# Projection pieces moved from behind the scores to the end of an attention step

## The chip, the cores and the metric

One core of a Trainium2 chip runs the kernel, in float32. The metric is device time in microseconds (us). TensorE multiplies (its weight loads run beside it), VectorE (DVE) and ScalarE (ACT) work on vectors, SyncE's queue (SP) starts the loads of the large weights, and GpSimd's queue (POOL) those of some small parameters. Each engine works through its own instructions in order and waits on semaphores for the others.

## What is computed

Two transformer layers run over 256 latent tokens and 256 context tokens of width 1024. The part that matters here is the token mixer of a layer:

```python
p = h @ w_in[l]                       # 2560 columns: q, k, v, u, g
s = einsum('bqhmd,bkhmd->bhmqk', q, k) * scale
pr = softmax(s)                       # two maps per head
w = pr[:, :, 0] - lam * pr[:, :, 1]
a = einsum('bhqk,bkhe->bqhe', w, v)   # then RMS norm per head
mixed = einsum('gpq,bcqge->bcpge', w_s, layernorm(g)) + b_s
o = concat([a, u * mixed]) @ w_out[l]
```

Beside it, modulation vectors `silu(c) @ ada_w[l]` are needed, then a dense SwiGLU (layer 0) or a mixture of 8 experts (layer 1).

## The kernel before

**Stages.** The work goes layer by layer: norm, projection of q, k and v, attention, output projection, feed-forward part or experts. Weights come as units of 512 KB through a ring of 8 buffers (`raw`). ScalarE rounds a unit to `w_hi` (L897), VectorE makes the rest `w_lo` (L1196), and each product is made of three matmuls (L493 to L495, helper `mm3`).

**Attention steps.** `attend(l)` exists once for each engine, as a software pipeline over steps t. An item is a pair of a block of 128 queries and a head: 16 items in layer 0 and 8 in layer 1. In layer 0 the first 8 items are of context queries with 256 keys ("short" here), all others have 512 keys ("long"). The loop has two steps more than items. In step t TensorE does, in this order:

1. the scores of item t (L641), which wait for both exponentials of item t-1, since there is one pair of banks for scores
2. `project_ug(l, t)`: half of the projection of one block of u or g, 12 matmuls (L493 to L495)
3. the turn of the modulation chunk of step t-1 (L530 for gates, L534 for others), which waits for the copy `arow`
4. the transposes of the weights of item t-1 (L659), which wait for VectorE's `weights`
5. the product of item t-2 with v (L669)
6. the rows of the modulation chunk of step t (`ada_rows`, L519); if the chunk before was a gate chunk of layer 0, they wait until it is finished on VectorE (L1242, L1243)
7. in some steps a mix of the spatial gating (L624)

Modulation chunks stand in 14 of the 16 steps of layer 0 (not in 7 and 15) and in 6 of the 8 of layer 1 (not in 3 and 7).

VectorE does in step t: the softmax weights of item t-1 (L1380 to L1383), the row maximum of item t (L1389, L1390), the finish of the chunk of step t-1, the copy of the product of item t-2 (L1397), in two steps of each layer the `w_lo` of two units, the copy `arow` of the chunk of step t (L1232), which waits for its rows, and then in some steps a gate (L1366), layer norm statistics (L1330, L1331), a spatial norm (L1338 to L1341) or a head norm with a root on ScalarE (L1438 to L1448). ScalarE copies a finished block of u or g (L1015) at the start of every other step, then does the exponentials of item t (L1022), in two steps the `w_hi` of two units, the copy of the transposed weights (L1033) and a square (L1040).

GpSimd's queue loads the bias and gain of the next gate chunk (`ab_bc`, `pg_bc`) once the gate chunk before is finished. SyncE's queue gives the next 512 KB unit to a ring buffer once its old unit was used. The loads of the experts' weights start when layer 1's attention is normed (semaphore `cat1`).

Of the kernel before, what the change touches and what calls it, by code (L numbers as in the profile page):

```python
# [95 lines left out]
def spread(t, c0, c1, steps):  # L96

    c = c0 + -(-t * (c1 - c0) // steps)
    return c if 0 <= t < steps and -(-(t + 1) * (c1 - c0) // steps) > c - c0 else None


def ada_slot(l, t):

    if l == 0:
        return spread(t, 4, ADA_L1, NB * HEADS)
    return spread(t, ADA_L1, 24, NLAT * HEADS)
# [60 lines left out]
def program(nc, x, c, ctx, c_ctx, ada_w, ada_b, pre_mix_g, post_mix_g, pre_ffn_g, post_ffn_g, w_in, w_out,  # L167
# [6 lines left out]
    with ExitStack() as stack:  # L174
        def sem(name):
            return stack.enter_context(nc.semaphore(name))
# [102 lines left out]
        def sg(name):  # L279

            if name not in S:
                S[name] = sem(name.replace(" ", "_"))
            return S[name]

        def view(ring, u):
            return ring.rearrange("p (k n) -> p k n", k=u.shape[0])
# [26 lines left out]
        def out_blocks(l):  # L313
            return range(NB) if l == 0 else range(NLAT)
# [176 lines left out]
        def _(pe):  # L491
            def mm3(o, lh, ll, rh, rl, start, stop):
                pe.matmul(o, lh, rh, start=start, stop=False)  # L493
                pe.matmul(o, lh, rl, start=False, stop=False)  # L494
                return pe.matmul(o, ll, rh, start=False, stop=stop)  # L495

            def split_at(s):
                return w_hi[:, s % SPL, :], w_lo[:, s % SPL, :]
# [7 lines left out]
            def ada_rows(c, bank, which=range(4)):  # L506

                if c and which[0] == 0:
                    if two_gates(c - 1):
                        pe.wait_ge(sg("ada fin"), c)  # L510
                    else:
                        pe.wait_ge(sg("arow"), c)
                for u in [at["ada", c][i] for i in which]:
                    pe.wait_ge(raw_in[u.k % RAW], raw_count(u.k))
                    w = view(raw_at(u.k), u)
                    for kk in range(2):
                        k = 2 * (u.a % 4) + kk
                        q = k % 4
                        m = pe.matmul(ps[32 * q:32 * q + 32, bank, :], cstat[:, k, :], w[:, kk, :],  # L519
                                      start=(k < 4), stop=(k >= 4), tile_position=(0, 32 * q))  # L520
                    m.then_inc(ada_used, 1)

            def ada_turn(c, bank):

                pe.wait_ge(sg("arow"), c + 1)
                if c:
                    pe.wait_ge(sg("ada fin"), c)
                if ADA_SEQ[c][1] in (2, 5):
                    for r in streams(ADA_SEQ[c][0]):
                        m = pe.matmul(ps[:, bank + 1 - r, :], cst[:, C_SELB + P * r:C_SELB + P * r + P], arow[:, :],  # L530
                                      start=True, stop=True)
                else:
                    for j in range(4):
                        m = pe.matmul(ps[:, bank + 1, 2 * j:2 * j + 2], arow[:, P * j:P * j + P], cst[:, C_SELC:C_SELC + 2],  # L534
                                      start=True, stop=True)
                m.then_inc(sg("ada post"), 1)
# [48 lines left out]
            def spatial_weights(l):  # L585

                pe.wait_ge(sg("ws in"), 16 * (l + 1))
                for g in range(4):
                    m = pe.transpose(ps[:, BANK_MIX, P * g:P * g + P], ws_raw[:, P * g:P * g + P], ident)
                m.then_inc(sg("wsT ps"), 1)  # L590

            def project_ug(l, f):

                c = f // 2
                nb = len(out_blocks(l))
                j, b = ug[l][c]
                bank = BANK_UG + c % 2 if c < nb else BANK_UG
                if f == 0:
                    pe.wait_ge(sg("qkT%d" % l), len(qk[l]))
                elif f == 2:  # L600
                    pe.wait_ge(sg("wsT"), l + 1)
                elif f % 2 == 0:
                    pe.wait_ge(sg("proj%d" % l), proj_n[l][2] + (c if c > nb else c - 1))
                for u in at["in", l, j][2 * (f % 2):2 * (f % 2) + 2]:
                    pe.wait_ge(lo_done, u.s + 1)
                    h, lo = (view(t, u) for t in split_at(u.s))
                    for kk in range(2):
                        k = 2 * at["in", l, j].index(u) + kk
                        m = mm3(ps[:, bank, :], hT_hi[:, k, P * b:P * b + P], hT_lo[:, k, P * b:P * b + P],
                                h[:, kk, :], lo[:, kk, :], k == 0, k == KD - 1)  # L610
                    if b == out_blocks(l)[-1]:
                        m.then_inc(unit_used, 1)
                if b < out_blocks(l)[-1]:
                    if f % 2:
                        m.then_inc(sg("ug part"), 1)

            def mix(l, i):

                b = out_blocks(l)[i]
                pe.wait_ge(sg("vn%d" % l), i + 1)  # L620
                if i:
                    pe.wait_ge(sg("gated"), NB * l + i)
                for g in range(4):
                    m = pe.matmul(ps[:, BANK_MIX, P * g:P * g + P], wsT[:, P * g:P * g + P],  # L624
                                  proj[:, b, 4 * DA + P * g:4 * DA + P * g + P], start=True, stop=True)
                m.then_inc(sg("mixed"), 1)

            def attend(l):
                its = items[l]
                n = len(its)  # L630
                for t in range(n + 2):
                    if t < n:
                        b, h = its[t]
                        k0 = 0 if b < NLAT else 256
                        if t == 0:
                            pe.wait_ge(sg("proj%d" % l), proj_n[l][1] + 2)
                            pe.wait_ge(sg("qkT%d" % l), len(qk[l]) if l else len(qk[l]) - 2 * NLAT)
                        else:
                            pe.wait_ge(sg("exp%d" % l), 2 * t)
                        for m_ in range(2):  # L640
                            m = pe.matmul(ps[:, m_, 0:512 - k0], qT[l][HD * m_:HD * m_ + HD, h, P * b:P * b + P],  # L641
                                          kT[HD * m_:HD * m_ + HD, h, k0:512], start=True, stop=True)
                        m.then_inc(sg("scores%d" % l), 1)
                        project_ug(l, t)
                    if t == 0:
                        spatial_weights(l)
                    if ada_slot(l, t - 1):
                        ada_turn(ada_slot(l, t - 1), ADA)
                    if 1 <= t <= n:
                        i = t - 1  # L650
                        b, h = its[i]
                        nk = 4 if b < NLAT else 2
                        pe.wait_ge(sg("weights%d" % l), i + 1)
                        if i:
                            pe.wait_ge(sg("wT%d" % l), i)
                        else:
                            pe.wait_ge(sg("proj%d" % l), proj_n[l][2])
                        for kb in range(nk):
                            m = pe.transpose(ps[:, BANK_W, P * kb:P * kb + P], pr[:, i % 2, 0, P * kb:P * kb + P], ident)  # L659
                        m.then_inc(sg("wT ps%d" % l), 1)  # L660
                    if t >= 2:
                        i = t - 2
                        b, h = its[i]
                        kb0, nk = (0, 4) if b < NLAT else (2, 2)
                        pe.wait_ge(sg("wT%d" % l), i + 1)
                        if i:
                            pe.wait_ge(sg("o%d" % l), i)
                        for kb in range(nk):
                            m = pe.matmul(ps[:, BANK_O, 0:P], wT[:, i % 2, P * kb:P * kb + P],  # L669
                                          proj[:, kb0 + kb, 2 * DA + P * h:2 * DA + P * h + P], start=(kb == 0), stop=(kb == nk - 1))  # L670
                        m.then_inc(sg("pv%d" % l), 1)
                    if ada_slot(l, t):
                        ada_rows(ada_slot(l, t), ADA)
                    if t in MIX_AT[l]:
                        mix(l, MIX_AT[l].index(t))
# [982 lines left out]
```

## Time and profile before

| what | value |
|---|---|
| median of 3 runs | 1927.09 us (1927.06 to 1927.76) |
| profiled execution, its time and its span | 1922.89 us, 1921.0 us |
| mean granted TensorE clock | 0.962 |
| TensorE busy | 1768.6 us (92%) |
| VectorE busy | 1331.0 us (69%) |
| ScalarE busy | 1099.1 us (57%) |

The span runs from the first to the last instruction. A share of busy time is a mean over all stages. Attention of layer 0 runs from 130 to 275 us, that of layer 1 from 786 to 863 us.

### The profile page before, as it was taken

How to read it: one execution, taken by the hardware profiler on the slowest of the kernel's cores; microseconds unless marked ns; L12 is line 12 of the kernel's file. 1: busy time of each engine (PE TensorE's matmuls, PEld its weight loads, DVE VectorE, ACT ScalarE, POOL GpSimd, SP SyncE). 2: the span in 40 equal slices, each digit the busy share in tenths (PEclk: the TensorE clock that was granted, in tenths of full speed). 3: DMA queues.
4: the chain of work that ended last, by engine and by line, in shares of the span. 5: the costliest groups of instructions: out<-in, count | busy, mean ns of one | idle time of the engine just before them, and what ended most of it. 6: DMA issues, size and time to landing. Idle time of an engine off the chain costs nothing.

```text
span 1921.0 us, 24495 instructions
## 1 busy us (share of the span) xinstructions
PE 1768.6 (92%) x8208; PEld 1412.8 (74%) x8208; DVE 1331.0 (69%) x1595; ACT 1099.1 (57%) x1408; POOL 26.6 (1%) x45
## 2 busy tenths in 40 slices
PE   5899988999999979978599999999999999999993
PEld 1775567788888857646488888888888888888883
DVE  1445765443333455474599999999999999999994
ACT  2333434322222244344487888878888888888883
POOL 2000000000000000000000000000000000000000
PEclk7899999999999989997799999999999999999997
DMA  9438762534443323564599999999999999999992
GB/s 310 154 121 278 254 208 88 182 125 162 134 132 99 95 59 99 175 208 154 196 394 371 376 388 359 395 368 381 383 362 394 366 381 389 360 394 363 382 384 91
DMA packets 232655, 504.91 MB, mean 263 GB/s; under 512 B 15672, under 2 KB 38352, under 8 KB 232320
## 3 DMA queue, kind: packets, MB, share of 16 engines
q1 hardware_dynamic: 229312, 493.49, 71.3%
q0 software_dynamic: 3264, 10.39, 1.9%
q8 instruction: 46, 0.75, 0.2%
q14 instruction: 33, 0.27, 0.0%
HBM read 496.48 MB, written 19.92 MB: 269 GB/s over the span
## 4 chain that ended last, share of the span: by engine, by line
issue 52%; PE 37%; DVE 6%; DMA 2%; ACT 2%; POOL 0%; SPq 0%; POOLq 0%; ACTq 0%; DVEq 0%
PE ps L493 11%; PE ps L495 10%; PE ps L494 10%; PE ps L519 2%; DMA raw<-in_ada_w 1%; DVE w_lo L1196 1%; DMA pg_bc<-in_post_ffn_g 1%; PE ps L641 1%; PE ps L669 1%; PE ps L534 1%; PE ps L543 1%; DVE xs L1309 1%; DVE hT_lo L1283 0%; DVE gg L1243 0%; DVE gg L1242 0%
## 5 line engine op out<-in xcount | busy, mean ns | idle before, releaser
L1196 DVE TENSOR_TENSOR w_lo<-raw,w_hi 128x1024 fp32r<-128x1024 f32 x570 | 685.2, 1223 | 298.6 <-ACT w_hi L897 264.2
L1109 ACT ACTIVATE w_hi<-raw 128x1024 fp32r<-128x1024 f32 x448 | 473.8, 1061 | 106.7 <-PE ps L495 106.7
L493 PE MATMUL ps<-w_hi,he_hi 128*128 128x512 f32 x896 | 354.6, 396 | 0.7 <-DVE he_lo L1528 0.7
L495 PE MATMUL ps<-w_hi,he_lo 128*128 128x512 f32 x896 | 350.4, 391 | 0.0
L494 PE MATMUL ps<-w_lo,he_hi 128*128 128x512 f32 x896 | 349.8, 390 | 0.0
L1196 DVE TENSOR_TENSOR w_lo<-raw_more,w_hi 128x1024 fp32r<-128x1024 f32 x224 | 273.9, 1225 | 45.7 <-ACT w_hi L1109 26.3
L1109 ACT ACTIVATE w_hi<-raw_more 128x1024 fp32r<-128x1024 f32 x224 | 237.8, 1063 | 53.5 <-PE ps L495 53.5
L897 ACT ACTIVATE w_hi<-raw 128x1024 fp32r<-128x1024 f32 x122 | 128.7, 1063 | 214.3 <-PE ps L495 214.3
L495 PEld LDWEIGHTS ps<-w_hi,he_lo 128*128 128x128 f32 x896 | 168.8, 188 | 36.1
L493 PEld LDWEIGHTS ps<-w_hi,he_hi 128*128 128x128 f32 x896 | 169.0, 189 | 34.9 <-issue 1.0
L494 PEld LDWEIGHTS ps<-w_lo,he_hi 128*128 128x128 f32 x896 | 169.0, 189 | 33.9
L493 PE MATMUL ps<-w_hi,ae_hi 128*128 128x512 f32 x448 | 175.2, 391 | 5.6 <-DVE ae_lo L1547 5.6
L495 PE MATMUL ps<-w_hi,ae_lo 128*128 128x512 f32 x448 | 174.4, 389 | 0.0
L494 PE MATMUL ps<-w_lo,ae_hi 128*128 128x512 f32 x448 | 174.4, 389 | 0.0
L493 PE MATMUL ps<-w_hi,hT_hi 128*128 128x512 f32 x368 | 151.0, 410 | 22.2 <-DVE hT_lo L1427 6.6
L494 PE MATMUL ps<-w_lo,hT_hi 128*128 128x512 f32 x368 | 146.7, 399 | 0.0
L495 PE MATMUL ps<-w_hi,hT_lo 128*128 128x512 f32 x368 | 146.6, 398 | 0.0
L493 PE MATMUL ps<-hT_hi,w_hi 128*128 128x512 f32 x352 | 137.8, 391 | 6.0 <-DVE hT_lo L1283 6.0
L494 PE MATMUL ps<-hT_lo,w_hi 128*128 128x512 f32 x352 | 137.7, 391 | 0.0
L495 PE MATMUL ps<-hT_hi,w_lo 128*128 128x512 f32 x352 | 137.6, 391 | 0.0
L493 PEld LDWEIGHTS ps<-w_hi,hT_hi 128*128 128x128 f32 x368 | 71.5, 194 | 54.0 <-issue 24.0
L493 PEld LDWEIGHTS ps<-w_hi,ae_hi 128*128 128x128 f32 x448 | 84.1, 188 | 24.8 <-issue 3.4
(206 smaller groups left out, 1950.3 us busy)
## 6 DMA issues: line engine op xcount, KB each, us to landing
raw<-in_moe_w SPq DMA_DIRECT2D x448, 512.0 KB, 6.1
raw_more<-in_moe_w SPq DMA_DIRECT2D x224, 512.0 KB, 6.1
raw<-in_ada_w SPq DMA_DIRECT2D x96, 512.0 KB, 6.0
raw<-in_ffn_w SPq DMA_DIRECT2D x66, 512.0 KB, 3.8
raw<-in_w_in SPq DMA_DIRECT2D x40, 512.0 KB, 3.8
raw<-in_w_out SPq DMA_DIRECT2D x16, 512.0 KB, 7.7
yrows<-in_x SPq DMA_DIRECT2D x8, 512.0 KB, 6.8
xe<-xrows SPq DMA_DIRECT2D x8, 512.0 KB, 6.6
```

Source lines behind the costliest of these rows:

```text
L493: pe.matmul(o, lh, rh, start=start, stop=False)
L494: pe.matmul(o, lh, rl, start=False, stop=False)
L495: return pe.matmul(o, ll, rh, start=False, stop=stop)
L519: m = pe.matmul(ps[32 * q:32 * q + 32, bank, :], cstat[:, k, :], w[:, kk, :], start=(k < 4), stop=(k >= 4), tile_position=(0, 32 * q))
L534: m = pe.matmul(ps[:, bank + 1, 2 * j:2 * j + 2], arow[:, P * j:P * j + P], cst[:, C_SELC:C_SELC + 2], start=True, stop=True)
L543: m = pe.transpose(ps[:, k, P * b:P * b + P], xn[:, b, P * k:P * k + P], ident)
L641: m = pe.matmul(ps[:, m_, 0:512 - k0], qT[l][HD * m_:HD * m_ + HD, h, P * b:P * b + P], kT[HD * m_:HD * m_ + HD, h, k0:512], start=True, s ...
L669: m = pe.matmul(ps[:, BANK_O, 0:P], wT[:, i % 2, P * kb:P * kb + P], proj[:, kb0 + kb, 2 * DA + P * h:2 * DA + P * h + P], start=(kb == 0) ...
L897: act.activation(w_hi[:, u.s % SPL, :], raw_at(u.k), ACT.Copy).then_inc(hi_done, 1)
L1109: act.activation(w_hi[:, s % SPL, :], expert_raw(i), ACT.Copy).then_inc(hi_done, 1)
L1196: dve.tensor_tensor(w_lo[:, s_ % SPL, :], src, w_hi[:, s_ % SPL, :].bitcast(F32), ALU.subtract)\
L1309: dve.scalar_tensor_tensor(out=xs[:, b, :], in0=src[:, b, :], scalar=st[:, 28 + b:29 + b], in1=xs[:, b, :], op0=ALU.mult, op1=ALU.add).the ...
```

## The change

In every step but step 0 of a layer, TensorE's piece of the projection of u and g (12 matmuls) is issued behind the product with v instead of behind the scores. In step 0 it stays. Nothing changes on the other engines, and no instruction is added or removed.

```diff
                         m.then_inc(sg("scores%d" % l), 1)
+                    if t == 0:
                         project_ug(l, t)
-                    if t == 0:
                         spatial_weights(l)
                     if ada_slot(l, t - 1):
                         ada_turn(ada_slot(l, t - 1), ADA)
...
                         m.then_inc(sg("pv%d" % l), 1)
+                    if 1 <= t < n:
+                        project_ug(l, t)
                     if ada_slot(l, t):
                         ada_rows(ada_slot(l, t), ADA)
                     if t in MIX_AT[l]:
```

## Rows read from the trace of the kernel before

**Rows 1.** Windows: stretch, busy us of PE, PEld, DVE, ACT, POOL, then clock, DMA.

```profile
125.00:330.00 205.00, 181.52 (x1026) 126.29 (x1025) 124.37 (x288) 78.56 (x193) 5.03 (x9) 0.98 0.61 209
...
900.00:1921.00 1021.00, 966.29 (x4377) 799.89 (x4375) 895.08 (x837) 789.22 (x829) 7.75 (x8) 0.97 0.95 353
```

**Rows 2.** Timeline of TensorE, steps 4 and 7 of layer 0: start us, us, instruction.

```profile
165.76 0.70 PE L641 MATMUL ps<-kT,qT 64*128 64x256 f32 x4
166.39 0.50 PE L493 MATMUL ps<-w_hi,hT_hi 128*128 128x512 f32 x1
...
169.24 0.95 PE L534 MATMUL ps<-cst,arow 128*128 128x2 f32 x8
170.05 0.41 PE L659 MATMUL ps<-cst,pr 128*128 128x128 f32 x2
...
190.07 1.88 PE L530 MATMUL ps<-arow,cst 128*128 128x512 f32 x4
```

**Rows 3.** Timeline of VectorE in the same step 4.

```profile
165.92 0.69 DVE L1232 COPY arow<-ps 128x512 f32<-128x512 f32 x1 [1.62 <-PE ps L519]
...
167.35 0.48 DVE L1383 SCALAR_TENSOR_TENSOR pr<-pr,att 128x256 f32<-128x256 f32 x1
```

**Rows 4.** Waits of TensorE from 130 to 863 us: who for whom, us, times, longest.

```profile
PE ps L659 <- DVE pr L1383: 8.1, 4, 5.7
PE ps L519 <- DVE gg L1243: 6.8, 3, 2.6
PE ps L493 <- DVE w_lo L1196: 4.2, 3, 2.5
...
PE ps L493 <- ACT proj L1015: 2.8, 2, 1.6
```

**Rows 5.** Windows behind four waits of TensorE: the clock stands after POOL.

```profile
147.00:149.00 2.00, 2.00 (x18) 0.56 (x15) 0.12 (x1) 0.00 (x0) 1.08 (x2) 1.00 0.18 57
...
196.20:199.40 3.20, 3.19 (x8) 2.52 (x9) 3.09 (x6) 0.00 (x0) 0.65 (x1) 0.50 0.76 212
...
211.90:216.30 4.40, 4.40 (x21) 0.92 (x21) 1.66 (x7) 2.73 (x7) 1.07 (x2) 0.64 1.00 318
...
855.30:859.00 3.70, 2.82 (x12) 2.53 (x12) 0.83 (x4) 1.00 (x3) 0.00 (x0) 0.60 0.00 0
```

**Rows 6.** Timeline of TensorE, step 13 of layer 0.

```profile
240.55 1.13 PE L641 MATMUL ps<-kT,qT 64*128 64x512 f32 x4
...
246.23 0.66 PE L659 MATMUL ps<-cst,pr 128*128 128x128 f32 x4 [0.80 <-DVE pr L1383]
...
249.56 1.16 PE L624 MATMUL ps<-proj,wsT 128*128 128x128 f32 x8
```

**Rows 7.** Timeline of VectorE: statistics, head norm, then step 13 of layer 0.

```profile
173.47 0.68 DVE L1330 BATCH_NORM_STATS2 st<-proj 128x6 f32<-128x512 f32 x1
...
174.40 0.17 DVE L1380 RECIPROCAL att<-att 128x2 f32<-128x2 f32 x1
...
180.41 0.16 DVE L1438 TENSOR_SCALAR st<-st 128x4 f32<-128x4 f32 x1
...
182.32 0.16 DVE L1380 RECIPROCAL att<-att 128x2 f32<-128x2 f32 x1
...
241.32 1.12 DVE L1366 SCALAR_TENSOR_TENSOR proj<-ps,pcol,proj 128x128 f32<-128x128 f32 x4
242.36 0.15 DVE L1338 RECIPROCAL st<-st 128x1 f32<-128x1 f32 x1
...
244.46 0.16 DVE L1380 RECIPROCAL att<-att 128x2 f32<-128x2 f32 x1
...
245.43 0.75 DVE L1383 SCALAR_TENSOR_TENSOR pr<-pr,att 128x512 f32<-128x512 f32 x1
```

**Rows 8.** The page's costliest groups: busy us, mean ns of one.

```profile
L1196 DVE TENSOR_TENSOR w_lo<-raw,w_hi 128x1024 fp32r<-128x1024 f32 x570 | 685.2, 1223 | 298.6 <-ACT w_hi L897 264.2
```

**Rows 9.** DMA issues from 140 to 160 us: KB each, us from issue to landing.

```profile
pg_bc<-in_post_mix_g POOLq DMA_DIRECT2D x1, 256.0 KB, 6.3
```

## The prediction

> **What bounds the kernel now.** I read the windows by stage first. In the attention stage of layer 0 TensorE is busy for 181.5 of 205 us, VectorE for 124.4, ScalarE for 78.6 [rows 1]. So TensorE sets the pace there, and time is won or lost only where it waits. I then read its timeline step by step. A step of layer 0 is dense: scores 0.63 us to the next instruction, projection 2.85, turn 0.81 [rows 2], then transposes, product with v and rows of the chunk. What matters is where VectorE stands meanwhile. It copies `arow` 0.16 us into the step, since the chunk's rows end the step before, and its last instruction of the softmax weights ends 2.07 us into the step (167.83 less 165.76) [rows 2, 3]. The transposes need these weights. Now they come at 4.29 us, behind the projection, and find them ready. The list of TensorE's waits shows what is left: 6.8 us for a gate chunk's finish, 8.1 for weights, 4.2 for `w_lo`, 2.8 for ScalarE's copy of a block of u or g [rows 4].
>
> **What the change removes.** The same waits, part by part.
> - The gate's finish (6.8 us in steps 1, 2 and 9 of layer 0): the turn now comes ahead of the projection, so VectorE finishes the gate under 2.85 us of projection.
> - `w_lo` and the copy of u or g (4.2 + 2.8 us): the projection that needs them starts later.
> - The weights in the steps behind the last item, and the two small ones (8.1 us): the last projection now stands right ahead of these transposes. What is left of them I count as new.
> - Three of these waits dropped the granted clock: 3.2 us at 0.50, 4.4 us at 0.64, 3.7 us at 0.60 [rows 5], which cost 1.6 + 1.6 + 1.5 = 4.7 us of full speed.
>
> Sum removed: 6.8 + 8.1 + 4.2 + 2.8 + 4.7 = 26.6 us. Work of TensorE, VectorE and ScalarE is the same, instruction for instruction.
>
> **What it adds: a wait for the weights in nearly every step.** In front of the transposes now stand only scores and turn. If W is the time from the start of the step to the end of the weights, TensorE waits W less scores and turn. Scores and turn are 0.63 + 0.81 = 1.44 us in a short step and 1.13 + 0.81 = 1.94 in a long one, where the scores take 1.13 [rows 2, 6]; a gate turn of layer 0 takes 1.88 instead of 0.81 [rows 2]. VectorE can't come earlier: the weights of item t-1 are queued behind `arow`, whose rows are still the last but one thing of the step before, and behind whatever small job stands after `arow`.
>
> W is put together from VectorE's rows. Base: 2.07 us short; long 2.5 (arow 0.16 + 0.6, then 246.18 less 244.46 = 1.72) [rows 3, 7]. Jobs between `arow` and the weights: statistics 0.93, head norm 1.91, gate 1.04, spatial norm 2.10 [rows 7]. A mix at the end of the step before hides 1.16 [rows 6].
>
> Layer 0, wait of TensorE in us:
> - steps 3 and 5 (statistics): 3.0 - 1.44 = 1.6 each; step 4: 0.6; step 6 (head norm): 4.0 - 1.44 = 2.5; step 7 (statistics, gate turn): 3.0 - 0.63 - 1.88 = 0.5
> - step 2: weights ready, but the next gate's parameters aren't. They are asked for when the first gate is done, 2 us ahead of the step by then, and take 6.3 us [rows 9] and their issue; then the gate takes about 2.6 us, while the rows could start at 6.2: 1.5
> - step 8: VectorE has a gate, two `w_lo` (1.22 us each [rows 8]) and the weights ahead: W about 3.8, no turn: 2.7. Step 9 has two more `w_lo`, statistics and a gate turn: W about 4.1, less 3.0, and 0.3 for its gate: 1.4
> - step 10 (head norm): 4.4 - 1.94 = 2.5; step 11 (spatial norm): 4.6 - 1.94 = 2.7; step 12 (norm less mix): 1.5; step 13 (gate and norm): 5.6 - 1.94 = 3.7; step 14 (norm and head norm less mix): 3.4; step 15 (gate): 1.6
>
> Sum: 1.5 + 1.6 + 0.6 + 1.6 + 2.5 + 0.5 + 2.7 + 1.4 + 2.5 + 2.7 + 1.5 + 3.7 + 3.4 + 1.6 = 27.8 us. Step 13 can be checked against today's trace: the transposes wait for the weights there already, for 0.80 us behind 2.85 of projection [rows 6]; 0.80 + 2.85 = 3.65.
>
> Layer 1: steps 1 and 2: 0.6 each; 3 (statistics): 1.5; 4 (two `w_lo`, no turn): 2.7; 5: 1.6; 6 (head norm): 2.5; 7 (norm): 2.7; 8: 1.5 of today's 5.7. Sum 13.7 us. Together 41.5 us.
>
> **The clock.** Behind waits of 2.5, 2.0 and 5.7 us the clock fell; behind the longest gate wait, 2.6 us, it stayed at 1.00 [rows 5]. Nine of the new waits are 2.4 us or longer (steps 6, 8, 10, 11, 13, 14; in layer 1 steps 4, 6, 7). The rows leave open which of them cost; the bounds are none of nine (0) and all (9 x 1.6 = 14.4 us). I take half, 7.2, since of the three rows in that size (2.0, 2.5, 2.6) two fell and one did not.
>
> **Queues.** No DMA moves in its queue. Ring buffers of u and g units come free later by 2 to 4 us; their successors are output weights and chunks that are used a step or more later. GpSimd's parameter loads start earlier, with the gates. Costed at nothing; if the cover were gone, what is shown for step 2 is the size. ScalarE's copy of u or g starts later but still ahead of the exponentials, and the exponentials end about 3 us behind the weights, while TensorE has product, projection and rows, over 5 us, to do.
>
> **Sum.** 41.5 + 7.2 - 26.6 = 22.1 us slower. The profiled execution would go from 1922.9 to 1945.0 us, its span from 1921.0 to 1943.1. The median shown is 4.2 us above the profiled execution; on it the forecast is 1927.1 + 22.1 = 1949 us. The experts' stage passes the delay on whole: its loads are started by the end of layer 1's attention (`cat1`), and TensorE is busy for 966 of 1021 us [rows 1].
>
> **Rivals.**
> - *The clock falls behind every wait of 1.4 us or more.* Against it: the clock stood at 1.00 behind 2.6 us. For it: a wait in each step is a new pattern, which no row shows. Then 9 more waits count and the other half of the nine: 13.5 x 1.6 = 22 us more, 1971 us. The Trainium skill (TensorE: Matmul & The Clock Gate, "A second HAM failure mode: psum-queue depth-cycling") tells of a kernel in which frequent short pauses between groups of matmuls made the clock swing between its levels; by that rule this rival holds, and the trace of before neither shows nor excludes it. Chance 0.08.
> - *Faster: VectorE reaches the weights ahead of its side jobs.* If each new wait were only its base (0.6 us; 2.7 in the two steps with `w_lo` and no turn, 1.5 in step 2), the new waits would be about 19 us against 26.6 removed: 1919 us. It decides where the mean new wait of some 22 steps falls below 1.2 us. For it: W is read from one schedule, and gates are finished earlier in the new one. Against: each side job waits for something behind `arow` or stands behind it in program order. Chance 0.05.
> - *Hidden later.* The delay goes into slack of the experts' stage, where DMA engines are busy for 0.95 of the time [rows 1], 1927 us. Against: those loads start with the delayed signal, and their work is not shortened. Chance 0.03.
>
> **How the numbers follow.** The likeliest case has 0.84. Its ends: no clock loss and 3 us less of new waits, 1927.1 + 41.5 - 3 - 26.6 = 1939; all nine losses and 3 us more, 1927.1 + 41.5 + 3 + 14.4 - 26.6 = 1959. I put the range at 1938 to 1962, a little into the clock rival, which leaves about 0.18 outside. A measurement can tell 0.2% (3.9 us) from no change. Slower: 0.84 + 0.08 = 0.92; same 0.03; faster 0.05.
>
> **What would show it.** TensorE's waits at L659 for `pr` of L1383 rise from 8.1 to some 38 us, in about 20 places, the largest (3.7 us) in step 13 of layer 0. Those at L519 for the gate fall from 6.8 to about 2, those of L493 in the steps for `w_lo` and the copy to nothing. Step 4 of layer 0 grows from 6.9 to 7.6 us, step 1 shrinks by 2.7. The mean clock in both attention stages falls. Layer 0's attention ends some 15 us later, layer 1's adds 5 to 10, and the stages between and after keep their length. The forecast is wrong if the weights end earlier in the step than 2 us short or 2.5 long, if the clock follows another rule than half of the long waits, or if the stages behind change.

## The result, and the profile after

| | before | changed |
|---|---|---|
| median | 1927.07 us (4 runs, 1926.53 to 1927.76) | 1949.31 us (4 runs, 1948.11 to 1955.09) |
| ratio | | 1.0121, 95% interval 1.0100 to 1.0142 |
| span of the profiled execution | 1921.0 us | 1946.6 us |

The kernel became slower by 22.2 us; 22.1 was forecast. The interval of the ratio reaches from 19 to 27 us, so an agreement to 0.1 us is chance. The line numbers of the changed kernel are 2 higher from the new lines on (L1385 is L1383 of before, L1245 is L1243, L1234 is L1232).

Where the 25.6 us between the two profiled executions lie is seen in windows that end at the same instructions: the first scores of layer 0, its first output projection, the first scores of layer 1, its first output projection, the end. (The first window begins 0.4 us earlier in the changed kernel.) The changed kernel (window, length, busy us of PE, PEld, DVE, ACT, POOL, clock, DMA):

```profile
129.90:300.90 171.00, 138.04 (x773) 88.98 (x773) 94.59 (x236) 57.59 (x150) 5.01 (x9) 0.92 0.63 214
300.90:808.90 508.00, 478.48 (x2120) 395.57 (x2120) 226.03 (x303) 164.51 (x248) 0.00 (x0) 0.97 0.37 117
808.90:892.30 83.40, 65.60 (x372) 40.05 (x372) 51.82 (x112) 34.12 (x80) 3.20 (x6) 0.97 0.60 202
892.30:1946.60 1054.30, 994.69 (x4493) 822.88 (x4493) 914.30 (x874) 802.91 (x857) 8.62 (x9) 0.96 0.94 348
```

The same windows of the kernel before:

```profile
130.30:279.60 149.30, 128.67 (x773) 82.56 (x773) 95.17 (x236) 57.90 (x150) 5.03 (x9) 0.98 0.71 245
279.60:786.00 506.40, 476.83 (x2122) 394.46 (x2122) 226.12 (x303) 164.56 (x248) 0.00 (x0) 0.98 0.37 118
786.00:867.00 81.00, 66.19 (x373) 42.20 (x373) 52.35 (x112) 34.48 (x80) 3.21 (x6) 0.95 0.60 208
867.00:1921.00 1054.00, 993.87 (x4493) 822.23 (x4493) 914.37 (x874) 802.65 (x856) 8.65 (x9) 0.97 0.94 348
```

Layer 0's attention takes 21.7 us more, layer 1's 2.4, the stage between 1.6 and the experts 0.3. VectorE's and ScalarE's busy time is unchanged; TensorE's rose by 9.4 us in layer 0 at the same 773 matmuls. Most of that is the clock: 0.98 before, 0.92 now. The rest stands around the waits, where an instruction counts as busy a little longer (step 4 below).

How much of such a difference is chance can be read from the experiments, where the same code was profiled again. Layer 1's attention with unchanged code took 81.0 us in the kernel before and 83.2 in the one that is late in layer 0 only. The stage between took 506.4 us before and 511.7 in the one that is late in layer 1 only, whose code up to there is that of before. So the 2.4 and 1.6 us are within what one execution differs from another, and the 21.7 us are far beyond it (unchanged code: 149.3 and 150.0).

The list of TensorE's waits from 130 to 885 us of the changed kernel (who for whom, us, times, longest) answers to [rows 4]:

```profile
PE ps L659 <- DVE pr L1385: 34.4, 21, 3.6
...
PE ps L519 <- DVE gg L1245: 1.5, 1, 1.5
...
PE ps L534 <- DVE arow L1234: 0.8, 4, 0.2
PE ps L530 <- DVE arow L1234: 0.4, 2, 0.2
```

The waits for the weights rose from 8.1 to 34.4 us, those for a gate fell from 6.8 to 1.5, and the lines for `w_lo` and for ScalarE's copy of u or g are gone. Step 4 of layer 0, TensorE and then VectorE, answers to [rows 2] and [rows 3]:

```profile
163.78 0.70 PE L641 MATMUL ps<-kT,qT 64*128 64x256 f32 x4
164.69 1.05 PE L534 MATMUL ps<-cst,arow 128*128 128x2 f32 x8 [0.21 <-DVE arow L1234]
165.91 0.44 PE L659 MATMUL ps<-cst,pr 128*128 128x128 f32 x2 [0.17 <-DVE pr L1385]
166.19 0.61 PE L669 MATMUL ps<-proj,wT 128*128 128x128 f32 x4
166.55 0.48 PE L493 MATMUL ps<-w_hi,hT_hi 128*128 128x512 f32 x1
...
171.34 0.70 PE L641 MATMUL ps<-kT,qT 64*128 64x256 f32 x4
```
```profile
163.94 0.69 DVE L1234 COPY arow<-ps 128x512 f32<-128x512 f32 x1 [4.37 <-PE ps L519]
...
165.38 0.48 DVE L1385 SCALAR_TENSOR_TENSOR pr<-pr,att 128x256 f32<-128x256 f32 x1
```

VectorE keeps its times within the step: `arow` 0.16 us in, the weights end 2.08 us in. But now the transposes stand at 2.13 us instead of 4.29, and so they wait. The step takes 7.56 us instead of 6.93. The profile lists 0.38 us as idle (0.21 and 0.17); the other 0.25 us are counted as busy, around two restarts of TensorE.

Step 14 is of the worst kind, with two side jobs ahead of the weights. Its VectorE rows show the queue: norm, then head norm, then the weights, which end at 273.73; the transposes start at 273.79:

```profile
268.01 0.15 DVE L1340 RECIPROCAL st<-st 128x1 f32<-128x1 f32 x1
...
270.11 0.16 DVE L1440 TENSOR_SCALAR st<-st 128x4 f32<-128x4 f32 x1
...
272.02 0.16 DVE L1382 RECIPROCAL att<-att 128x2 f32<-128x2 f32 x1
...
272.98 0.75 DVE L1385 SCALAR_TENSOR_TENSOR pr<-pr,att 128x512 f32<-128x512 f32 x1
```
```profile
269.38 1.05 PE L534 MATMUL ps<-cst,arow 128*128 128x2 f32 x8
273.79 1.11 PE L659 MATMUL ps<-cst,pr 128*128 128x128 f32 x4 [3.35 <-DVE pr L1385]
274.69 1.92 PE L669 MATMUL ps<-proj,wT 128*128 128x128 f32 x8
276.26 0.77 PE L493 MATMUL ps<-w_hi,hT_hi 128*128 128x512 f32 x1
277.39 0.40 PE L493 MATMUL ps<-w_hi,hT_hi 128*128 128x512 f32 x1
```

What follows the wait is slow: transposes 1.11 us instead of 0.66 [rows 6], a matmul of the projection 0.77 instead of 0.50 [rows 2], until the clock is back.

### The profile page after: what moved, and what is told of

It is laid out like the page before. It is cut to its first block, busy times and chain, and to the rows that moved or that the text cites. A ratio compares the mean times of both kernels' runs of the same rounds, so it can differ in the third digit from the quotient of the medians.

```text
span 1946.6 us, 24495 instructions
## 1 busy us (share of the span) xinstructions
PE 1778.9 (91%) x8208; PEld 1418.7 (73%) x8208; DVE 1329.7 (68%) x1595; ACT 1098.6 (56%) x1408; POOL 26.5 (1%) x45
## 4 chain that ended last, share of the span: by engine, by line
issue 51%; PE 37%; DVE 7%; DMA 2%; ACT 2%; POOL 0%; SPq 0%; POOLq 0%; ACTq 0%; DVEq 0%
PE ps L493 10%; PE ps L494 10%; PE ps L495 10%; PE ps L519 2%; DMA raw<-in_ada_w 1%; PE ps L669 1%; DVE pr L1385 1%; DVE w_lo L1198 1%; PE ps L659 1%; PE ps L543 1%; DVE xs L1311 1%; DVE pr L1384 0%; DVE arow L1234 0%; DVE hT_lo L1285 0%; PE ps L772 0%
## 5 line engine op out<-in xcount | busy, mean ns | idle before, releaser
L493 PE MATMUL ps<-w_hi,hT_hi 128*128 128x512 f32 x368 | 153.4, 417 | 15.2 <-DVE hT_lo L1429 6.6
L1024 ACT ACTIVATE pr<-ps,att 128x512 f32<-128x512 f32 (+1 forms) x48 | 29.2, 613 | 123.3 <-DVE att L1392 123.3
```

Of the source, the lines that this page charges most:

```text
L1024: act.activation(pr[:, t % 2, m_, 0:nk], ps[:, m_, 0:nk], ACT.Exp, scale=SCALE, bias=att[:, t % 2, 2 + m_:3 + m_], accum_out=att[:, t % 2, ...
```

## The experiments

All ratios are to the kernel before, run again beside each group of experiments (medians 1926.7 to 1927.4 us). Diffs are shown against the changed kernel.

**One layer at a time.** The late projection in layer 0 only, then in layer 1 only:

```diff
-                    if t == 0:
+                    if t == 0 or (l == 1 and t < n):      # l == 0 in the second kernel
                         project_ug(l, t)
...
-                    if 1 <= t < n:
+                    if 1 <= t < n and l == 0:             # l == 1 in the second kernel
                         project_ug(l, t)
```

> The projection stands late in layer 0 only, as in the changed kernel, and behind the scores in layer 1. The theory (new waits for the weights, step by step, and clock losses behind them) puts 21.8 us of the changed kernel's 24 us into the attention of layer 0, of which some 10 are clock: 1945 to 1949 us. If the loss came as much from layer 1, or from the stages behind, it would be 1938 or less.

> The projection stands late in layer 1 only. The theory: 12.1 us of new waits against 9.8 us of removed waits and clock behind the wait of 5.7 us: 1928 to 1931 us. If a late projection costs what it costs in layer 0 for each step (1.3 us), 1938 us.

Measured: layer 0 alone 1948.74 us (ratio 1.0107, 1.0087 to 1.0126); layer 1 alone 1927.52 us (1.0005, 0.9994 to 1.0016). The first is inside its band. The second lies 0.5 us below it and can't be told from no change. So the loss is layer 0's. In layer 1 the removed waits pay for the new ones to within about 3 us, the upper end of the interval.

**Only where a gate was waited for.** Steps 1, 2 and 9 of layer 0:

```diff
+LATE = ((0, 1), (0, 2), (0, 9))
...
-                    if t == 0:
+                    if t == 0 or (t < n and (l, t) not in LATE):
                         project_ug(l, t)
...
-                    if 1 <= t < n:
+                    if (l, t) in LATE:
                         project_ug(l, t)
```

> The projection stands late only in steps 1, 2 and 9 of layer 0, where the rows of a chunk wait for a gate. The theory: step 1 shorter by 2.7 us, step 2 by 0.4 (the next gate's parameters come late), step 9 about the same with 1.9 us of new wait against 2.0 removed, and the clock loss of 1.5 us behind it gone: 1922 to 1924 us. The rival that a late projection always costs: above 1927 us.

Measured 1922.62 us, ratio 0.9978 (0.9966 to 0.9989), as expected. A late projection isn't bad by itself: here it gives back the gate's wait. Step 1 takes 7.35 us there against 10.06 before, the 2.7 us expected; step 2 takes 8.92 against 10.08, where 0.4 us less was expected.

**Only where the new wait is longest.** The same with `LATE = ((0, 13),)`:

> The projection stands late in step 13 of layer 0 alone, the step with the longest new wait. The theory: the wait at the transposes grows from 0.8 to 3.6 us (2.8 more) and takes the clock with it or not (0 or 2 us); the next step's 1.6 us wait for the copy of u stays: 1929 to 1932 us. The rival that a delay in one step is taken up by slack in the next ones: 1927 us.

Measured 1928.91 us, ratio 1.0007 (0.9998 to 1.0017). The timeline has the wait that was forecast:

```profile
245.74 1.11 PE L661 MATMUL ps<-cst,pr 128*128 128x128 f32 x4 [3.57 <-DVE pr L1387]
```

But the medians differ by only 1.5 us, so the times can't decide between the forecast and no change; the 12 runs reach from 1927.17 to 1934.46 us, and the profiled one is the slowest of them. In that execution step 13 takes 15.68 us instead of 10.10 and layer 0's attention 154.2 instead of 149.3, so the steps behind took up 0.7 us of 5.6. It is one execution, with a clock loss behind the wait.

**The clock, with the waits kept.** 118 matmuls with unused results, 1 to 14 in a step (table `FILL`, not shown), stand in front of the waits for the weights and write into the bank that the transposes overwrite. (The expectation says 119; the table adds up to 118, 83 in layer 0 and 35 in layer 1.)

```diff
-                        pe.wait_ge(sg("weights%d" % l), i + 1)
...
+                        for _ in range(FILL.get((l, t), 0)):
+                            pe.matmul(ps[:, BANK_W, :], hT_hi[:, 0, 0:P], hT_hi[:, 0, 0:512], start=True, stop=True)
+                        pe.wait_ge(sg("weights%d" % l), i + 1)
```

> The changed kernel with 119 idle matmuls (128x128 by 128x512, into the bank that the transposes overwrite) in front of the waits for the weights, 1 to 14 in a step, so many that they end before the weights come. The waits stay, TensorE is just busy in them. The theory that about 10 us of the changed kernel's time are clock losses: 1939 to 1943 us, granted clock of the attention of layer 0 near 0.98. If the clock costs nothing: 1949 us or more.

Measured 1939.78 us, ratio 1.0060 (1.0043 to 1.0077), as expected. More work on the engine that bounds the stage made the kernel 9.5 us faster than the changed one. The window over layer 0's attention, and the wait that is left:

```profile
131.30:291.40 160.10, 147.67 (x856) 93.67 (x856) 94.30 (x236) 57.46 (x150) 5.01 (x9) 1.00 0.67 229
```
```profile
PE ps L662 <- DVE pr L1388: 6.0, 15, 1.5
```

The stage takes 160.1 us instead of 171.0, at a clock of 1.00 instead of 0.92 (1.00 is the upper of the engine's two levels, 2.4 GHz). So the changed kernel loses some 10 us to the clock: 9.5 by the medians, 10.9 by the stage. That is its whole clock loss, not what the change added: the kernel before lost some 4.7 us too, by the prediction's count from [rows 5]. So of the 22.2 us some 5 are clock and some 17 waiting, both net of what was removed. This split is an estimate, since the intervals of the two ratios are each some 3 to 4 us wide to either side.

**The side jobs behind the weights.** Statistics, spatial norm, head norm (all but its mean) and gate move behind the next row maximum:

```diff
+                def side(t):
+                    if t in GATE_AT[l]:
+                        gate(l, GATE_AT[l].index(t))
...
                         dve.tensor_scalar(att[:, p, 2:4], att[:, p, 0:2], -SCALE, None, ALU.mult).then_inc(sg("rowmax%d" % l), 1)
+                    if t:
+                        side(t - 1)
```

> The changed kernel; VectorE does the side jobs (statistics, spatial norm, head norm, gate of u) behind the next row maximum instead of ahead of the weights. The theory: each new wait falls to its base (0.6 us in long steps, 1.4 less than the scores and turn in short ones; the steps with w_lo keep theirs), some 23 us less of waits and most clock losses gone: 1915 to 1922 us. The rival that the transposes wait for something else (the exponentials, ScalarE): 1945 us or more.

Measured 1918.57 us, ratio 0.9958 (0.9946 to 0.9970). The waits for the weights fall to a third:

```profile
PE ps L659 <- DVE pr L1404: 11.6, 17, 2.9
```

So what the transposes waited for was, for the most part, the side jobs ahead of the weights in VectorE's queue.

**The weights under the late projection.** VectorE makes the weights of item t at the end of step t, ahead of `arow`, not at the start of step t+1. First on the changed kernel, then on the kernel before:

```diff
-                    if 1 <= t <= n:
-                        i = t - 1
+                    if t < n:
+                        i = t
                         p = i % 2
...
                     if ada_slot(l, t):
                         ada_copy(ada_slot(l, t), ADA)
```

(The block stands at the head of the step in the one and right ahead of the last two lines in the other.)

> The changed kernel; VectorE makes the weights of item t at the end of step t, ahead of the copy of the chunk's rows, so under the late projection. The theory: all new waits go and the removed ones stay removed, 1900 to 1908 us. The rival that the wait only moves (to the exponentials or to the turn's arow copy): 1925 us or more.

> The kernel before with the same move of the weights alone. The theory: the weights bind before only in steps 13 and 15 and in the steps behind layer 1's last item, so 1921 to 1926 us, while gate and w_lo waits stay. If the weights' place helps by itself as much as with the late projection: 1908 us or less.

Measured 1912.79 us, ratio 0.9924 (0.9904 to 0.9944), 5 us above its band; and 1923.93 us, ratio 0.9983 (0.9972 to 0.9993), as expected. What the first missed is in its timeline. In step 1 the turn waits for `arow`, which now stands behind the weights (first line). In steps 7 and 8 the weights stand behind the two `w_lo`, and the transposes of step 8 wait for them (second line):

```profile
140.38 1.98 PE L530 MATMUL ps<-arow,cst 128*128 128x512 f32 x4 [1.25 <-DVE arow L1234]
...
194.91 0.44 PE L659 MATMUL ps<-cst,pr 128*128 128x128 f32 x2 [2.05 <-DVE pr L1400]
```

The pair says what the change itself is worth. With the weights early, the late projection gains 11.1 us (1923.93 to 1912.79); with the weights at the head of the next step it loses 22.2.

**The weights ahead of `w_lo` too,** in step 0 behind `arow`, on the changed kernel, and the same with the projection between turn and transposes. `weights(i)` is the block that stood at the head of the step; its removal there is not shown:

```diff
+                    if 1 <= t < n:
+                        weights(t)
                     if t in (2 * nb - 1, 2 * nb):
                         split_upto(at["in", l, IN_ORDER[4]][2 * (t - (2 * nb - 1)) + 1].s)
                     if ada_slot(l, t):
                         ada_copy(ada_slot(l, t), ADA)
+                    if t == 0:
+                        weights(t)
```

> The changed kernel; VectorE makes the weights of item t at the end of step t and ahead of the w_lo units too, in step 0 behind the copy of the chunk's rows. The kernel with the weights ahead of the rows' copy alone still waits 1.3 us in step 1, 2.1 in step 8 of layer 0 and 2.3 and 1.2 in steps 4 and 5 of layer 1, with clock losses behind two of them. The theory: these go, 1904 to 1908 us. If the w_lo units are then late instead: 1911 us or more.

> The same early weights, with the projection between the turn and the transposes. With the weights out of the way the place behind the turn and the place at the end differ only where the projection waits for w_lo (step 8 of layer 0, 4 and 5 of layer 1: 1 to 2 us each, perhaps with a clock loss): 1908 to 1914 us.

Measured 1907.52 us, ratio 0.9895 (0.9880 to 0.9910), and 1916.33 us, ratio 0.9939 (0.9924 to 0.9954), 2 us above its band. The first is the fastest kernel of this study. One wait of size is left in the steps of its layer 0, in step 9, where `arow` is queued behind two `w_lo`:

```profile
200.00 1.98 PE L530 MATMUL ps<-arow,cst 128*128 128x512 f32 x4 [2.61 <-DVE arow L1234]
```

The second waits 4.0 us for `w_lo` in two places and 4.4 us for the weights (0.2 and 1.4 us in the first), and its clock over the two attentions is 0.97 and 0.91 instead of 1.00 and 0.97.

**Between turn and transposes,** with VectorE as before:

```diff
                     if ada_slot(l, t - 1):
                         ada_turn(ada_slot(l, t - 1), ADA)
+                    if 1 <= t < n:
+                        project_ug(l, t)
                     if 1 <= t <= n:
...
-                    if 1 <= t < n:
-                        project_ug(l, t)
```

> The projection stands between the turn and the transposes in every step but 0. The weights keep their cover, the gate gets it too. The theory: step 1 shorter by 2.7 us, step 2 by 0.4, step 9 by 2.0 and 1.5 of clock behind it, five short steps longer by 0.3 each (the turn waits for arow): 1921 to 1923 us. The rival that any move away from the scores costs: above 1927 us.

Measured 1921.95 us, ratio 0.9972 (0.9960 to 0.9984), as expected in time. Step 9 did not go as told: its turn waits 2.45 us for `arow` and its rows 1.00 for the gate, and it takes 12.07 us against 11.11; step 8 lost its wait for `w_lo` instead (7.20 us against 10.63).

## Why the prediction was right

**The new waits.** W, the time from a step's start to the end of its weights, was the key number, and it holds: 2.08 us in step 4 (2.07 forecast), 5.41 in step 14. The listed idle times sum to 34.4 for the weights, 1.5 for the gate and 1.2 for `arow`, 37.1 us against 41.5. But the sum was made of whole gaps between instructions, and the listed idle is less: step 4 grew by 0.63 us (0.6 forecast) with 0.38 listed, step 3 by 1.54 (1.6) with 1.33. About 0.12 us for each of 28 waits closes 3.4 of the 4.4 us. Most single waits came 0.1 to 0.3 us below the forecast. Step 9 fell furthest short (0.52 us at the transposes against 1.4); only step 2 came out longer, by its 0.2 us for `arow`. The longest is 3.56 us in step 13 (3.7 forecast).

**The removed waits** went as the sum had them: the gate's to 1.5 us, all of it in step 2 for want of the next parameters (1.5 forecast), those for `w_lo` and the copy to nothing, the 5.7 us wait in layer 1 to 1.40 (1.5 forecast). The exact 1.5 in step 2 is partly chance: in the kernel that is late in layer 0 only the same wait took 0.86 us. These waits were summed as listed, without the 0.12 us each; for 12 of them that is 1.4 us more.

VectorE's row in step 2 shows what the gate waited for:

```profile
150.62 0.69 DVE L1244 TENSOR_TENSOR gg<-ps,ab_bc 128x512 f32<-128x512 f32 x1 [2.14 <-DMA pg_bc<-in_post_mix_g]
```

**The clock.** The term was 7.2 us; the filler measured 9.5. The size was near, the rule behind it (half of the long waits) was not. In layer 0 the clock fell behind all six long waits and in step 5 besides, in layer 1 behind none of three. There the matmuls behind the 2.43 us wait of step 4 keep their usual length:

```profile
844.47 0.66 PE L659 MATMUL ps<-cst,pr 128*128 128x128 f32 x4 [2.43 <-DVE pr L1385]
...
845.77 0.48 PE L493 MATMUL ps<-w_hi,hT_hi 128*128 128x512 f32 x1
```

The Trainium skill (TensorE: Matmul & The Clock Gate, "A second HAM failure mode: psum-queue depth-cycling") describes a clock that swings under frequent short pauses. This trace agrees in part, with 0.92 over layer 0's attention, and disagrees in layer 1, where eight waits of 0.4 to 2.5 us left it at 0.97, above the 0.95 of before.

**Where the total is luck.** The forecast had layer 0's attention end some 15 us later and layer 1's add 5 to 10, with a lower clock in both. Measured are 21.3 us later and 2.4 more, and layer 1's clock rose; the kernels with one layer changed say the same (21.6 us and 0.4 above before). The clock rule is the main reason: it gave six of its nine long waits to layer 0 and three to layer 1, at half the price each, and the runs have the whole price in layer 0 and nothing in layer 1. In the sum the two errors cancel in part. The rest is made up by the terms: new waits 40.5 us with the 0.12 us each (41.5 forecast), clock 9.5 (7.2), removed 26.6 + 1.4. By this estimate, 40.5 + 9.5 - 28.0 = 22.0 us, the mechanism of waits and clock accounts for the loss.

**The rivals.** The clock rival (1971 us) fell: behind the waits of 1.44 and 1.46 us in steps 12 and 15 of layer 0 the matmuls keep their usual 0.47 us. The rival that ended faster was priced at 1919 us for the case that each new wait is only its base. It didn't hold. The kernel that makes its condition true by moving the side jobs ran in 1918.57 us, with 15.2 us of new waits listed (11.6 for the weights, 2.4 for the gate, 1.2 for `arow`) where the rival had about 19, so its price was near. "Hidden later" fell: the experts' stage took 1054.3 us instead of 1054.0. The stage between the layers grew by 1.6 us, which was not forecast; with unchanged code ahead of it the same stage took 511.7 us in another execution, so this is no sign of the change.

## What to carry to other kernels

A block of work on the bounding engine is also cover for whatever the next instruction waits for. Before it is moved, measure when that input is ready in the step, counting the whole queue ahead of it on the other engine. If the block is to move, move the producer under it as well: here the same edit costs 22 us or gains 11, by where VectorE makes the weights.

## What the runs showed that was not expected

The clock depends on more than the length of a wait. In step 5 of layer 0 the changed kernel and the one that is late in layer 0 alone have the same waits, 0.2 and 1.12 us. The window over the step, the changed kernel first:

```profile
171.30:181.40 10.10, 8.77 (x50) 5.80 (x46) 3.98 (x12) 2.87 (x8) 0.00 (x0) 0.83 0.61 208
```
```profile
173.40:181.90 8.50, 7.17 (x51) 4.46 (x47) 3.90 (x12) 2.87 (x8) 0.00 (x0) 1.00 0.73 252
```

Same instructions, same waits, 10.1 us at 0.83 in the one, 8.5 us at 1.00 in the other.

It differs even where all the code so far is the same. The first four microseconds of layer 0's output projection, behind the same wait of 2.39 us, in the kernel before and in the one that is late in layer 1 only:

```profile
279.50:283.50 4.00, 3.94 (x18) 3.31 (x19) 3.93 (x10) 1.29 (x2) 0.00 (x0) 1.00 0.82 237
```
```profile
279.70:283.70 4.00, 3.94 (x11) 3.10 (x12) 3.93 (x10) 1.30 (x2) 0.00 (x0) 0.59 0.78 226
```

The clock stayed at 1.00 in the one and read 0.59 in the other. So no rule that names only the length of a wait can tell which waits cost the clock; what decides it stays open here. It also means that the stages of two single executions can be compared only to a few microseconds.

And giving TensorE useless work in its waits won 9.5 us, since it kept the clock in layer 0's attention at its upper level.
